# Every second step of the state chain moved directly behind a step of the triangular inverse

## The reference, cut to what matters

```python
def step(S, inp):                      # per head, S is 64 x 64
    r_t, w_t, k_t, v_t, kk_t, b_t = inp
    sa = jnp.einsum('bhvk,bhk->bhv', S, -kk_t)
    S = S * w_t[:, :, None, :] + sa[..., None] * b_t[:, :, None, :] + v_t[..., None] * k_t[:, :, None, :]
    y = jnp.einsum('bhvk,bhk->bhv', S, r_t)
    return S, y
_, ys = lax.scan(step, S0, (tm(r), tm(decay), tm(k), tm(v), tm(kk), tm(b)))
```

## Time and profile before

| | |
|---|---|
| median of three executions | 1326.67 us |
| the profiled execution, its span on the engines | 1325.83 us, 1324.0 us |
| TensorE matmuls busy | 1287.6 us (97%) |
| VectorE, ScalarE, GpSimd busy | 723.1, 699.1, 306.6 us |
| mean granted TensorE clock | 0.993 |
| iterations with RWKV work (chain steps, L804) | 121.3 to 717.5 us |

### The profile page before, as it was taken

How to read it: one execution, slowest core, us unless ns; L and a number is a source line. 1 busy time by engine, 2 the same in 40 slices (tenths; PEclk the granted TensorE clock), 3 DMA queues, 4 the chain that set the end, 5 groups by cost and what they waited for, 6 DMA issues and landing times.

```text
span 1324.0 us, 24437 instructions
## 1 busy us (share of the span) xinstructions
PE 1287.6 (97%) x9453; PEld 1113.9 (84%) x9453; DVE 723.1 (55%) x1671; ACT 699.1 (53%) x1683; POOL 306.6 (23%) x234
## 2 busy tenths in 40 slices
PE   7999999999999999999999999999999999999996
PEld 7989798897979889798797878888898888778885
DVE  5356867768676776868664543334443445540013
ACT  6446767666666766667655543445344444432321
POOL 3430000010000101000002333433434334334443
PEclk8999999999999999999999999999999999999998
DMA  6322111211112121121212222222222222236333
GB/s 225 91 68 63 56 52 57 60 56 51 57 56 61 49 63 53 57 58 49 65 52 78 73 64 80 73 68 68 85 71 70 79 80 71 73 96 231 96 96 141
DMA packets 151523, 102.35 MB, mean 77 GB/s; under 512 B 6414, under 2 KB 140912, under 8 KB 149872
## 3 DMA queue, kind: packets, MB, share of 16 engines
q1 hardware_dynamic: 151408, 100.79, 25.6%
HBM read 96.57 MB, written 4.19 MB: 76 GB/s over the span
## 4 chain that ended last, share of the span: by engine, by line
PE 83%; DVE 7%; ACT 5%; issue 3%; DMA 1%; SPq 0%; POOL 0%; DVEq 0%; ACTq 0%
PE tile L598 49%; PE tile L884 2%; PE tile L886 2%; PE tile L885 2%; PE ma L854 2%; PE ma L720 1%; PE mb L869 1%; PE mb L804 1%; PE ma L729 1%; PE ma L884 1%; PE ma L886 1%; PE ma L885 1%; PE mb L884 1%; PE mb L886 1%; PE mb L885 1%
## 5 line engine op out<-in xcount | busy, mean ns | idle before, releaser
L598 PE MATMUL tile<-hn_hi,w_hi 128*128 128x264 f32 (+2 forms) x1664 | 435.8, 324 | 0.0
L598 PE MATMUL tile<-hn_hi,w_lo 128*128 128x264 f32 (+2 forms) x1664 | 429.0, 320 | 0.0
L598 PE MATMUL tile<-hn_lo,w_hi 128*128 128x264 f32 (+2 forms) x1664 | 426.5, 319 | 0.0
L1313 POOL TENSOR_TENSOR w_lo<-w_raw,w_hi 128x512 fp32r<-128x512 f32 x196 | 258.5, 1322 | 421.2 <-ACT w_hi L983 421.0
L598 PEld LDWEIGHTS tile<-hn_hi,w_hi 128*128 128x128 f32 x1664 | 270.4, 189 | 29.1 <-issue 11.3
L598 PEld LDWEIGHTS tile<-hn_hi,w_lo 128*128 128x128 f32 x1664 | 270.0, 189 | 13.7 <-issue 1.7
L983 ACT CAST w_hi<-w_raw 128x512 fp32r<-128x512 f32 x324 | 199.4, 616 | 155.3 <-PE tile L598 60.0
L598 PEld LDWEIGHTS tile<-hn_lo,w_hi 128*128 128x128 f32 x1664 | 269.8, 189 | 9.9 <-issue 0.2
L1328 POOL TENSOR_TENSOR arena<-arena,power 128x10 f32<-128x10 f32 (+3 forms) x28 | 44.2, 1579 | 577.1 <-DVE arena L1506 443.6
L1159 ACT ACTIVATE arena<-ma 64x192 f16<-64x192 f32 x240 | 77.9, 325 | 56.1 <-PE ma L720 54.6
L1168 ACT ACTIVATE arena<-ma 128x384 f16<-128x384 f32 x120 | 58.8, 490 | 68.5 <-PE ma L761 67.5
(11 more groups left out here) (257 smaller groups left out, 2169.5 us busy)
## 6 DMA issues: line engine op xcount, KB each, us to landing
w_raw<-w_in SPq DMA_DIRECT2D x260, 256.0 KB, 2.8
w_raw<-w_out SPq DMA_DIRECT2D x64, 256.0 KB, 3.0
big<-x SPq DMA_DIRECT2D x4, 1024.0 KB, 7.2
arena<-x SPq DMA_DIRECT2D x4, 1024.0 KB, 8.7
out<-big SPq DMA_DIRECT2D x3, 1024.0 KB, 3.9
arena<-post_norm_w SPq DMA_DIRECT2D x1, 1024.0 KB, 5.0
out<-big SPq DMA_DIRECT2D x2, 512.0 KB, 3.8
arena<-table_rope SPq DMA_DIRECT2D x2, 264.0 KB, 3.0
```

Source lines behind the costliest of these rows:

```text
L598: last = mm(o[:, at:at + n], w[:, slot, cols], t[:, kt, tok:tok + n], start=(kt == 0 and w is w_hi and t is hn_hi), stop=(kt == KT - 1 and ...
L1313: T(w_lo[:, slot, :], w_raw[:, slot, :], w_hi[:, slot, :].bitcast(F32), ALU.subtract).then_inc(s("lo_done"), 1)
```

## The change

One constant is added, and the chain's places are moved by it: a call with a step whose whole part is even comes 0.345 steps earlier. So steps 0, 2, 4, 6 and 8 stand at 4.355, 6.355, ... 12.355, which is 0.005 behind the x of levels 1 to 5, and steps 1, 3, 5 and 7 stay. The last chain group, which runs in the first attention iteration, is placed by another rule and keeps its places. No instruction is added or removed, and no wait; the instructions' line numbers are one higher in the changed kernel from L329 on.

```diff
-        CHAIN_FROM, CHAIN_STEP = 4.7, 1.0
+        CHAIN_FROM, CHAIN_STEP, BEHIND = 4.7, 1.0, 0.345
...
         def chain_at(g, step, late, work):
             if late and work == "attn":
                 return LATE_AT + LATE_STEP * step
-            return inv_at((g + 1) % NG, CHAIN_FROM + CHAIN_STEP * step)
+            whole = math.floor(step)
+            return inv_at((g + 1) % NG, CHAIN_FROM + CHAIN_STEP * step - (BEHIND if whole % 2 == 0 else 0))
```

## The result

The changed kernel takes 1354.39 us, the median of three executions (1353.59 to 1354.58), against 1326.67 before: 27.7 us more, a ratio of 1.0207 with a 95% interval of 1.0191 to 1.0223. The sign and the main mechanism are those of the prediction; the time is 8 us above its 1346 and 2.4 us above the end of its range. The profiled execution has a span of 1352.8 us. The granted TensorE clock is 1.00 all through the iterations with RWKV work in both traces. It has a part at one place behind them: from 770.2 to 773.6 us, in the attention part, it is 0.50 in the changed kernel (1.2 GHz, the lower of its two levels), and a projection pass starts every 0.44 us there instead of every 0.24. Both kernels stand idle for 2.0 us just ahead of that place, and only the changed kernel's trace has the slow stretch. It is worth 1.4 us of that one execution's span.

A forecast was written before the change was run, and what follows sets the result against it. The prediction saw a TensorE stream with few holes, where new waits are paid in full. ScalarE's holds less one gain summed to 19.7 us over the profiled 1325.83; with 0.84 for the median, 1346 us, range 1338 to 1352.

The forecast's parts named there:

- ScalarE's order as the cost: On ScalarE's in-order queue, chain copies awaiting later matmuls would hold back the copy of x; chance 0.81.
- rival D: ScalarE's casts of weights, delayed by the held queue, starve TensorE's passes: 17 us more, 1363 us; chance 0.03.
- T1: Group 2, step 4: ScalarE's copy of U delays cast, x copy and bank copies; 1.3 us, seven times, 9.1 us.
- T5: Group 0, step 4: ScalarE's copy of U goes ahead of the copy of x; 0.17 us, eight times, 1.4 us.
- T3: Group 1, step 4: U waits for G's copy, its ScalarE copy delays that of x; 0.44 us, eight times, 3.5 us.
- T2: Group 2, step 8: ScalarE's waiting output copy delays the copy of x; 0.64 us, seven times, 4.5 us.
- T4: Group 1, step 8: ScalarE's waiting output copy delays the copy of x; 0.43 us, eight times, 3.4 us.
- T6: Group 0, step 6: a gain, ScalarE's state scaling fills idle time and x starts 0.35 us earlier, seven times, -2.5 us.
- TensorE's own half at 0: At TensorE's 115 joins behind x, the moved matmuls save and cost nothing: 0 taken from 0 to -9.2 us.
- A: At TensorE's 115 joins, each saves 0.08 us of weight load, 9.2 us in all: 1317 to 1322 us; chance 0.03.
- B: ScalarE's holds are covered by the room between x and the next matmul needing it: 1324 to 1329 us; chance 0.03.
- C: Group 2, step 4: only the copy of x holds TensorE, not bank copies; 0.6 instead of 1.3 us, 1341.5; chance 0.10.

The follow-up runs named there:

- pe_only: The changed kernel with only TensorE's steps moved, ScalarE and VectorE in the order of the kernel before: 1330.79 us, ratio 1.0026.
- act_only: The kernel before with only ScalarE's copies moved as in the change, TensorE and VectorE in the old order: 1373.42 us, ratio 1.0348.
- act6: The kernel before with one edit, ScalarE's two step-6 state-scaling instructions put ahead of the copy of x: 1325.47 us, ratio 0.9987.
- pe_keeps6: The changed kernel with TensorE's step 6 (the third chunk's G) back at its old place behind L693: 1349.53 us, ratio 1.0172.
- pe_no6: The kernel before with only TensorE's steps 0, 2, 4 and 8 joined to x; step 6 and the other engines as before: 1329.30 us, ratio 1.0019.

## Why the prediction was right or wrong

- **What bounds the kernel, and ScalarE's order as the cost: right.** pe_only and act_only settle it. The three new holes and their releasers are as said, and the cast's delay cost nothing (rival D): no wait for a cast of ScalarE is among TensorE's. One sign did not come as said: the idle time of L1168 neither vanished nor named L809, but halved, and the wait for L809 stands on the copy ahead of it.
- **T1 to T5: right, and their sum nearly so.** What ScalarE's copies cost is what goes when they are put back. By the starts in the traces, iterations 1 to 8, the step-4 copies came to 13.7 us (T1, T3 and T5: 14.0 predicted) and the step-8 copies to 9.1 (T2, T4 and the last iteration: 8.2). The 13.7 hold some luck, since the misses cancel: T1 is 0.72 + 0.74 = 1.46 us against 1.3, T3 0.50 less 0.15 that is TensorE's own, 0.35 against 0.44, and T5 0.16 less 0.07, 0.09 against 0.17. T2 is 0.69 against 0.64 and T4 0.50 against 0.43, by the same subtraction. T1 was read too short in the lags: U behind L766 starts 0.63 us behind x and its copy 0.48 us later, where I took 0.55 and 0.42. In T4 the second matmul starts 0.45 us behind x, where I took 0.33: the pair is slower behind an f16 group, which lengthened the hold.
- **The failed step: T6.** "Moved ahead, they fill an idle stretch and the activations start 0.35 us earlier: x starts 0.35 earlier in iterations 1 to 7, -2.5 us (T6)." It was +0.19 instead, seven times, which is 1.3 us: 3.8 us between the two. Two things were wrong. I took ScalarE's queue as the only thing that the activations wait for, when L693's result was close behind it: with the queue clear, the gain is 0.25 and not 0.35 (act6), because 1.15 us behind the start of L693 is the earliest seen (299.03 after 297.87, 297.45 after 296.29; in act6 290.13 after 288.98). And I did not follow TensorE's half of the same step past L693, though the order of before and after shows G change sides with it. pe_keeps6 shows that this is the cause: it alone turns +0.19 into -0.25.
- **The second failed step: TensorE's own half at 0.** It costs 2.8 us beside T6 (pe_no6), above the bounds of 0 to -9.2 that I had drawn. That a join saves nothing was right, and by itself it costs little: 0 to 0.05 us where the joined matmul starts at once behind x. What I set at nothing is mostly the waits, which make 2.4 us in group 1's steps 0, 2 and 4. I had read that U of group 1's step 4 waits for VectorE's copy of G, and reckoned it for ScalarE alone; TensorE stands still too, 0.15 us. I had read that S of step 2 waits for U's copy, and let the next G's wait swallow it; it costs 0.07. And I erred the other way too: about 0.18 us per iteration came back at group 1's step 3, where the earlier S took away most of the wait that I had said would stay. The 7.5 us that I gave that wait was a misreading besides: it adds the matmuls' 1.9 us and their weight loads' 5.7.
- **Sum.** By the starts in the traces the iterations 1 to 8 grew by 27.0 us against 19.7 predicted. ScalarE's copies make 0.6 of the difference (22.8 against 22.2), T6 3.8 and TensorE's other steps 2.8: 7.2 of the 7.3. The timed difference of 27.7 is 0.7 above that, which is within what single executions differ by.
- **Rivals.** A (a join saves) does not show. B and D show in no view. C (the bank copies do not hold L720) would have had no wait of L721 for L1182; there are 5.6 us. The upper end, 1352, already had T6 absent; it had nothing for T6 turned round, and the 0.06 us that it adds for a wait with two semaphores is shown by no run.

The Trainium skill's rule that the queues of ScalarE and VectorE are strict first-in, first-out ("PSUM — Partial Sum Buffer", "Engine vs sequencer instructions") is what act_only shows best: the copy of x, ready long before, never passed the copy that waited, and some 38 us came of it in the iterations 1 to 8. Its rule for TensorE ("TensorE: Matmul & The Clock Gate", "Step-by-step: what each phase is for") is that only weight loads are pulled ahead and matmuls stay in program order. That is T6's failure in one sentence: G ahead of L693 makes L693 late by G's 0.44 us, and the trace agrees.

The difference of the two profiled spans is 28.8 us. The iterations 1 to 8 hold 27.0 of it, 0.35 lie before them, and 1.4 are the stretch at the lower clock at 770 us. What stays open is why the clock fell there and not in the kernel before, behind the same stop of 2.0 us (2.05 against 2.00), and what holds the load of G at group 1's step 0.

## What to carry to other kernels

When a step is placed nearer to a producer, move every engine's share of it on paper and ask of each what it now stands in front of. A reader that waits at the head of an in-order queue costs whatever is behind it, and the same step's matmul, put before another strand's producer, can undo a gain on a third engine. Readers belong behind the work that is ready sooner, even where the matmul that they read comes early: the same matmul order cost 3.7 us with the readers late and 27.7 with them early.

## What the runs showed of the hardware that was not expected

- A pair of f32 matmuls of 128 columns takes 0.44 us to the next start directly behind an f16 group (three of 64 columns), and 0.36 between two f32 passes. A pass behind such a group or such a pair takes 0.31 to 0.32 us, and 0.23 behind another pass. So joining the pair to the group moves the slow starts about and leaves their sum as it was, within 0.01 us at three of the places where the pair starts 0.11 us behind the group, and within 0.05 at all of them.
- Two stops of TensorE of 1.05 and 0.75 us, with one f16 group between them, were followed by 3.4 us at a granted clock of 0.50 in six iterations of seven (act_only, iterations 2 to 8, all but the last); stops of 0.54 and 0.75 us at the same place (the kernel after) never were. By the shifts it cost some 1.6 us each time, nearly as much as the stops.
- An instruction of 0.22 us that waited 1.24 us at the head of ScalarE's queue cost TensorE 1.46 us in each iteration, the sum of the two, though ScalarE is busy for only 52% of the span.
